# Another order for the prologue of a hybrid attention and MoE layer on eight cores

## The chip, the cores and the metric

The kernel runs on the 8 cores of one Trainium2 chip, all with the same program and each with its own part of the data. The cores don't wait for each other. The metric is the device time in microseconds (us) of the slowest core.

## What is computed

One layer, for 2 sequences of 8192 tokens of width 1024, conditioned by a vector `c` per sequence. The changed part prepares the first half of the layer:

```python
ada = jax.nn.silu(c) @ ada_w[l] + ada_b[l]                    # (B,6D)
sh1, sc1, g1, sh2, sc2, g2 = jnp.split(ada[:, None, :], 6, axis=-1)
h = rmsnorm(x, norm1_g[l]) * (1.0 + sc1) + sh1
proj = h @ w_in[l]                                            # (B,S,3072)
q, k, v, gb, gc, hc = jnp.split(proj, split_pts, axis=-1)
attn = diff_attention(q, k, v, positions, rel_bias, ...)      # causal, 2 softmax maps per head
conv = short_conv(gb, gc, hc, conv_w[l])
mix = jnp.concatenate([attn, conv], axis=-1) @ w_out[l]
x = x + g1 * mix
h = rmsnorm(x, norm2_g[l]) * (1.0 + sc2) + sh2
x = x + g2 * hier_moe(h, ...)
```

`rel_bias` gives each head a bias that depends only on the distance between query and key. It matters near the diagonal, and is applied there as a factor.

## The kernel before

Each core attends from 16 blocks of 128 own queries to all keys before them. It makes the keys (`KT`) and the values (`VA`) for its whole sequence itself, in 32 chunks of 256 tokens, and its queries in 8 chunks of 256. A chunk is a *unit*. The list `units` names them in order, and each has a place in one of three input buffers, `xb[u % 3]`. `load_unit(u + 3)` is issued on GpSimd's queue (POOL) when the last matmul of unit `u` is issued. Such a load casts float32 to bf16 on its way. `sq_unit(u + 1)` squares the next unit on VectorE (DVE) into the one tile `sq`, and is issued right behind the matmuls that take the statistics of unit `u` (`it_stat`), which read `sq`. So the place of a unit in the program also places the square of the next on DVE.

The order on each engine is that of the calls of `P.op`. An engine waits for the semaphores of an operation before it starts it, and everything behind it on that engine waits too. No planner moves anything.

The prologue is what comes before the first attention pair. In the program's order it is:

- SyncE's queue (SP) loads `ada_w` in pieces of 512 columns (`ada_ld`, two loads of 1 MB each). Pieces 2 and 3 make the scale `sc1`. Then come small tables, and the weights of keys and values into the staging tiles `wA` and `wB` (`w_ld`, 2 MB each).
- DVE multiplies pieces 2 and 3 with silu(c) (`gemv`, 8 operations a piece), and TensorE (PE) turns the result into columns (`to_cols`). The scale `der` comes of that.
- *Small tables*: DVE makes `rb0`, `Sm` and `c8`, PE multiplies them (`mmw`), ScalarE (ACT) takes the exponential, and DVE writes `w8b`. SP stores it to `wscr` in device memory. Then come lambda (`lamp`, `lams`), `identb` and a small memset on POOL.
- `cast_piece` scales `wA` and `wB` into `Wkv`, every second of the 16 slices on DVE and the others on ACT.
- SP loads the five *Hankel tiles* `Hs_l` from `wscr`: each has 128 partitions of 8 rows of 128 bf16, 256 bytes a row, with the start shifted by one element from partition to partition. Behind them on SP stand the *shift loads*: `ada_w` pieces 0 and 1 (for `sh1`), and the weights of the queries into `wA`.
- Keys and values of chunks 0 and 1, then `ada_piece(0)` and `ada_piece(1)` (the shift, which ends with the addition into `adaT`), chunk 2, `gq` (the shift times the query weights, for `bias_q`), the casts of `wA` into `Wq`, the keys of chunk 3, the five Hankel tiles through PE into `Mt`, `bias_q`, the queries of chunk 0, the values of chunk 3, and `gv` (for `bias_v`). Then the attention pairs begin.

In the tables below L344 is `ada_ld`, L348 `w_ld`, L328 `load_unit`, L332 `sq_unit`, L373 and L376 a `gemv`, L385 `to_cols`, L549 and L573 statistics and keys, L598 values, L632 and L655 statistics and projection of the queries, L450 and L454 the casts, L411 the first small table on DVE, L420 `mmw`, L467 the Hankel loads, L684 the addition into `adaT`, L702 the copies into `Mt`. L807, L815 and L818 are scores, exponential and the factor `Mt` of an attention pair.

## Time and profile before

| | |
|---|---|
| time, median of 3 runs | 1859.33 us (1854.24 to 1882.98) |
| the profiled execution's own time | 1857.9 us |
| its span, first to last instruction, slowest core (core 3) | 1856.4 us |
| spans of the eight cores | 1833.4 to 1856.4 us |
| busy on core 3: PE, DVE, ACT, POOL | 71%, 42%, 46%, 16% of the span |
| first attention scores on core 3 | at 119.58 us |

A time in the trace counts from the first instruction of its core. "Idle before, releaser" is how long an engine had waited, and for what. A row of SPq is the issue of a DMA, not its transfer. The prologue is the first 6% of the span, and everything after it is started by the attention loop.

### The profile page before, as it was taken

To read this page: it belongs to the slowest core of one execution; us is meant where nothing else is said; L and a number is where in the kernel's file an instruction comes from. 1 tells how busy PE (TensorE), PEld (TensorE's weight loads), DVE (VectorE), ACT (ScalarE), POOL (GpSimd) and SP (SyncE) were. 2 spreads that over 40 slices of the span, in tenths; PEclk is the share of its full clock that TensorE was granted. 3 is DMA by queue.
4 is the path that set the end of the run, shared out by engine and by line. 5 is a ranking of instruction groups with operands and counts; after the bars stand their busy time and mean duration, and the time that the engine had idled before them with its cause. 6 is when DMAs were issued, how large, how long until landed. Compare 5 with 4: busy or idle time off the path is not lost.

```text
span 1856.4 us, 41117 instructions; the slowest of 8 cores (1833.4 to 1856.4 us)
## 1 busy us (share of the span) xinstructions
PE 1311.5 (71%) x14526; PEld 880.3 (47%) x14526; DVE 779.5 (42%) x1229; ACT 846.6 (46%) x1122; POOL 303.3 (16%) x317
## 2 busy tenths in 40 slices
PE   1577777877888998899996268883156888888400
PEld 1354455565666676677775246661123433344200
DVE  4465455653333233223123377664612322233266
ACT  1134344555677887888885136652011221222122
POOL 0000000000000100001000043332311222222243
PEclk9788889999999999999998579996578999999855
DMA  8746556674455556656649844313158686421276
GB/s 224 187 94 140 115 121 136 151 174 64 80 80 96 94 87 95 102 84 100 95 78 199 227 131 128 103 58 108 68 191 288 215 287 212 165 90 37 92 230 222
DMA packets 120460, 252.88 MB, mean 136 GB/s; under 512 B 25643, under 2 KB 53019, under 8 KB 120264
## 3 DMA queue, kind: packets, MB, share of 16 engines
q0 software_dynamic: 30112, 96.50, 28.0%
q1 hardware_dynamic: 90152, 153.75, 26.5%
q8 instruction: 125, 2.05, 0.4%
q14 instruction: 71, 0.58, 0.1%
HBM read 400.89 MB, written 89.70 MB: 264 GB/s over the span
## 4 chain that ended last, share of the span: by engine, by line
PE 46%; issue 15%; DVE 13%; DMA 12%; ACT 10%; SPq 3%; POOL 1%; DVEq 0%; ACTq 0%; POOLq 0%
PE psd L838 9%; PE psd L1527 7%; ACT arena L815 6%; PE psd L573 5%; PE psd L598 5%; PE psd L807 5%; DMA wal<-wbf 5%; PE psd L1559 4%; PE psd L1204 2%; DMA arena<-w_in 2%; DMA arena<-ada_w 2%; DVE arena L1631 2%; PE psd L1165 1%; PE psd L655 1%; DVE arena L1185 1%
## 5 line engine op out<-in xcount | busy, mean ns | idle before, releaser
L815 ACT ACTIVATE arena<-psd,arena 128x1024 bf16<-128x1024 f32 x544 | 572.4, 1111 | 230.3 <-PE psd L809 214.3
L838 PE MATMUL psd<-arena 128*128 128x129 bf16 x4352 | 311.0, 226 | 12.4 <-DVE arena L818 10.1
L838 PEld LDWEIGHTS psd<-arena 128*128 128x128 bf16 x4352 | 283.7, 101 | 45.6 <-issue 14.7
L1527 PE MATMUL psd<-wal,arena 128*128 x752 | 195.5, 398 | 50.0 <-DMA wal<-wbf 30.9
L807 PE MATMUL psd<-arena 64*128 64x128 bf16 x2176 | 184.5, 218 | 28.5 <-ACT arena L815 22.1
L573 PE MATMUL psd<-arena 128*128 128x256 bf16 x1024 | 157.5, 292 | 45.5 <-ACT arena L557 18.9
L809 PE MATMUL psd<-arena 64*128 64x128 bf16 x2176 | 186.7, 219 | 0.4 <-issue 0.4
L807 PEld LDWEIGHTS psd<-arena 64*128 64x128 bf16 x2176 | 124.2, 94 | 104.4 <-issue 91.2
L598 PE MATMUL psd<-arena 128*128 128x512 bf16 x512 | 144.0, 385 | 30.6 <-DVE arena L611 10.9
L1527 PEld LDWEIGHTS psd<-wal,arena 128*128 128x128 bf16 x752 | 75.7, 101 | 169.3 <-issue 117.3
L1534 ACT ACTIVATE arena<-psd 128x512 f32<-128x512 f32 x47 | 28.1, 597 | 277.2 <-PE psd L1527 240.0
L481 POOL DMA_DIRECT2D wbf<-wex x96 | 50.0, 521 | 618.0 <-ACT arena L815 427.2
L611 DVE TENSOR_SCALAR arena<-psd,arena 128x512 bf16<-128x512 f32 x56 | 42.1, 752 | 234.5 <-PE psd L598 222.5
L573 PEld LDWEIGHTS psd<-arena 128*128 128x128 bf16 x1024 | 93.8, 104 | 76.4 <-issue 54.1
L809 PEld LDWEIGHTS psd<-arena 64*128 64x128 bf16 x2176 | 122.4, 95 | 1.6 <-issue 1.5
L1165 PE MATMUL psd<-arena 128*128 128x260 bf16 x768 | 99.3, 289 | 14.5 <-ACT arena L1170 12.2
L1559 PE MATMUL psd<-wal,arena 128*128 x376 | 88.7, 378 | 17.2 <-DVE arena L1547 15.2
L1547 DVE COPY arena<-psd 128x512 bf16<-128x512 bf16 x47 | 19.9, 424 | 180.2 <-PE psd L1544 150.8
L1570 POOL DMA_INDIRECT ysc<-arena x47 | 47.4, 1009 | 284.8 <-DVE arena L1567 273.4
L1567 DVE SCALAR_TENSOR_TENSOR arena<-psd,arena 128x1024 f32<-128x1024 f32 x47 | 60.3, 1284 | 76.0 <-PE psd L1559 74.5
L1165 PEld LDWEIGHTS psd<-arena 128*128 128x128 bf16 x768 | 77.1, 102 | 30.4 <-issue 15.2
L818 DVE TENSOR_TENSOR arena<-arena 128x1024 bf16<-128x1024 bf16 x79 | 53.1, 688 | 50.3 <-ACT arena L815 50.1
(222 smaller groups left out, 1585.7 us busy)
## 6 DMA issues: line engine op xcount, KB each, us to landing
wal<-wbf SPq DMA_DIRECT2D x300, 512.0 KB
wbf<-wex POOLq DMA_DIRECT2D x96, 512.0 KB, 5.5
arena<-ada_w SPq DMA_DIRECT2D x24, 1024.0 KB
arena<-xc POOLq DMA_DIRECT2D x32, 512.0 KB, 7.4
arena<-ysc SPq DMA_DIRECT2D x16, 1024.0 KB
arena<-w_in SPq DMA_DIRECT2D x12, 1024.0 KB
arena<-xo SPq DMA_DIRECT2D x16, 520.0 KB
arena<-xr SPq DMA_DIRECT2D x16, 512.0 KB
```

The source lines that it names most:

```text
L481: P.op("pool", lambda e: e.dma_start(out=wbf[pt][ex, :, :], in_=wex[ex, :, pt * PCW:(pt + 1) * PCW]), after=after, w=[("wbf", ex, pt)], dm ...
L573: ins = e.matmul(ps[:, m2 * 256:(m2 + 1) * 256], lhsT=Wkv[:, fc, mc * 128:(mc + 1) * 128], rhs=xbu[:, fc, :], start=(fc == 0), stop=(fc == ...
L598: ins = e.matmul(ps, lhsT=xbu[:, fc, t_ * 128:(t_ + 1) * 128], rhs=Wkv[:, fc, 512:1024], start=(fc == 0), stop=(fc == 7), skip_group_check ...
L807: e.matmul(sA[:, h * 128:(h + 1) * 128], lhsT=KT[0:64, h, kb * 128:(kb + 1) * 128], rhs=qt[0:64, h, q0:q0 + 128], start=True, stop=True)
L809: ins = e.matmul(sB[:, h * 128:(h + 1) * 128], lhsT=KT[64:128, h, kb * 128:(kb + 1) * 128], rhs=qt[64:128, h, q0:q0 + 128], start=True, st ...
L815: P.op("act", lambda e: e.activation(out=Pt[pb], in_=psd[sset][:, :], func=AF.Exp, scale=rk[:, kb:kb + 1]), r=[PSK(2 * sset), PSK(2 * sset ...
L818: P.op("dve", lambda e: e.tensor_tensor(out=Pt[pb], in0=Pt[pb], in1=Mt[:, gen, :], op=ALU.mult), r=[("Pt", pb), "Mt"], w=[("Pt", pb)])
L838: ins = e.matmul(omap(m), lhsT=Pt[pb][:, c * 512 + h * 128:c * 512 + (h + 1) * 128], rhs=VA[:, kb, h, :], start=(first and m % 3 == 0), st ...
L1165: ins = e.matmul(psb[bk][:, 0:260], lhsT=Wc[:, fc, br * 512 + cc * 128:br * 512 + (cc + 1) * 128], rhs=hnp[pp][:, fc, :, :], start=(fc == ...
L1527: ins = e.matmul(pd[:, :], lhsT=hT[b % 2][:, fc, :], rhs=ap_, start=(fc == 0), stop=(fc == 7))
L1559: ins = e.matmul(py[:, hf * 512:(hf + 1) * 512], lhsT=hidT[b % 2][:, jc, :], rhs=ap_, start=(jc == 0), stop=(jc == 3))
L1567: P.op("dve", lambda e: e.scalar_tensor_tensor(out=ysb[b % 2], in0=py[:, :], scalar=gateT[:, b:b + 1], in1=G2bc, op0=ALU.mult, op1=ALU.mul ...
```

## The change

Four things move, and no computation is added or taken away:

1. `cast_piece(wA)` and `cast_piece(wB)` stand ahead of the small tables, and the shift loads (`ada_ld(0, 0)`, `ada_ld(1, 2)`, `w_ld(wA, ...)`) right behind them.
2. The store to `wscr` and the five Hankel loads are issued by POOL instead of SP.
3. The first query chunk is the third unit instead of the fifth, and chunks 2 and 3 of the keys move back by one. Its statistics come ahead of the shift pieces, its projection right behind the Hankel tiles.
4. The casts into `Wq` are all on ACT (8) instead of 4 on DVE and 4 on ACT.

```diff
-    units = [("kv", c) for c in range(4)] + [("q", 0), ("q", 1)]
+    units = [("kv", 0), ("kv", 1), ("q", 0), ("kv", 2), ("kv", 3), ("q", 1)]
...
          r=["vec", "der"], w=["der"])
 
+    def cast_piece(stg, stgkey, dst, dcol, gcol, engs=("dve", "act"), width=512):
...
+    G1C = der[:, GSC1:GSC1 + 8]
+    cast_piece(wA, "wA", Wkv, 0, G1C)
+    cast_piece(wB, "wB", Wkv, 512, G1C)
...
+    ada_ld(0, 0)
+    ada_ld(1, 2)
+    w_ld(wA, "wA", 0)
     P.op("dve", lambda e: e.tensor_scalar(out=nb31, in0=nb31, scalar1=-1.0, scalar2=None, op0=ALU.mult),
          r=["nb31"], w=["nb31"])
...
-    P.op("sp", lambda e: e.dma_start(out=wscr[:, :], in_=w8b), r=["w8"], w=["wscr"], dma=True)
+    P.op("pool", lambda e: e.dma_start(out=wscr[:, :], in_=w8b), r=["w8"], w=["wscr"], dma=True)
...
-    G1C = der[:, GSC1:GSC1 + 8]
-    cast_piece(wA, "wA", Wkv, 0, G1C)
-    cast_piece(wB, "wB", Wkv, 512, G1C)
...
-        P.op("sp", lambda e, sp_=sp_, src=src: e.dma_start(out=Hs_l[sp_], in_=src), r=["wscr"], w=[("Hs", sp_)], dma=True)
-    ada_ld(0, 0)
-    ada_ld(1, 2)
-    w_ld(wA, "wA", 0)
+        P.op("pool", lambda e, sp_=sp_, src=src: e.dma_start(out=Hs_l[sp_], in_=src), r=["wscr"], w=[("Hs", sp_)], dma=True)
...
-    k2, v2 = kv_items(2, 2)
-    k3, v3_ = kv_items(3, 3)
-    for it in k0 + k1 + v0 + v1:
+    qi0 = q_items(2, 0)
+    k2, v2 = kv_items(3, 2)
+    k3, v3_ = kv_items(4, 3)
+    for it in k0 + k1 + v0 + v1 + qi0[0:1]:
         issue(it)
     ada_piece(0, 0)
     ada_piece(1, 2)
...
-    for it in k2 + v2:
-        issue(it)
     gq, _ = gemv(lambda kc: wA[:, kc, :], lambda kc: adaT[:, SH1 + kc:SH1 + kc + 1], lambda kc: ["wA", "adaT"])
-    cast_piece(wA, "wA", Wq, 0, der[:, GQ:GQ + 8])
-    for it in k3:
+    cast_piece(wA, "wA", Wq, 0, der[:, GQ:GQ + 8], ("act",))
+    for it in k2:
         issue(it)
     for sp_ in range(5):
...
-    for it in q_items(4, 0):
-        issue(it)
-    for it in v3_:
+    for it in qi0[1:] + v2 + k3 + v3_:
         issue(it)
```

The orders below are those of the two programs. In brackets stand the semaphores that an operation waits for: s_pe is PE's own count, and so on, and d with a number is one DMA's.

POOL before, from the third load of a unit on:

```order
L328 DMA arena<-xc 128x2048 [waits s_dve]
L444 MEMSET arena 128x32
L328 DMA arena<-xc 128x2048 [waits s_pe,d48]
L328 DMA arena<-xoq 128x2048 [waits s_pe,d49,s_dve]
L328 DMA arena<-xoq 128x2048 [waits s_pe,d50,s_dve]
```

POOL after, the same stretch, where L449 is the store to `wscr` and L470 the Hankel loads:

```order
L328 DMA arena<-xoq 128x2048 [waits s_dve]
L449 DMA wscr<-arena 8x768 [waits s_dve]
L465 MEMSET arena 128x32
L470 DMA arena<-wscr 128x8x128 [waits d51]
L470 DMA arena<-wscr 128x8x128 x4
L328 DMA arena<-xc 128x2048 [waits s_pe,d48]
L328 DMA arena<-xc 128x2048 [waits s_pe,d49,s_dve]
```

The load of unit 3 (the first that waits for s_pe) now stands behind six other DMAs in POOL's queue.

DVE before, from the last small table to the shift pieces, where L454 are the casts and L464 is `antib`:

```order
L443 CAST arena<-arena 128x128 [waits d13]
L454 TENSOR_SCALAR arena<-arena 128x512 [waits d14]
L454 TENSOR_SCALAR arena<-arena 128x512 x3
L454 TENSOR_SCALAR arena<-arena 128x512 [waits d15]
L454 TENSOR_SCALAR arena<-arena 128x512 x3
L464 CAST arena<-arena 128x128 [waits d12]
L332 TENSOR_TENSOR arena<-arena 128x2048 [waits s_pe,d49]
L332 TENSOR_TENSOR arena<-arena 128x2048 [waits s_pe,d50,s_dve]
L373 TENSOR_SCALAR arena<-arena 128x512 [waits d22]
```

DVE after, from the casts on (L419; L432 to L437 are the tables ahead of `mmw`, L448 is `w8b`):

```order
L419 TENSOR_SCALAR arena<-arena 128x512 [waits d15]
L419 TENSOR_SCALAR arena<-arena 128x512 x3
L432 TENSOR_SCALAR arena<-arena 8x1 [waits d10]
L434 TENSOR_TENSOR arena<-arena 32x8 [waits d8,d9]
L435 TENSOR_SCALAR arena<-arena 32x768 [waits d6,d7]
L437 TENSOR_SCALAR arena<-arena 8x768
L448 TENSOR_TENSOR arena<-arena 8x768 [waits s_act,s_dve]
...
L332 TENSOR_TENSOR arena<-arena 128x2048 [waits s_pe,d49]
L332 TENSOR_TENSOR arena<-arena 128x2048 [waits s_pe,d50,s_dve]
L332 TENSOR_TENSOR arena<-arena 128x2048 [waits s_dve,s_pe,d57]
L373 TENSOR_SCALAR arena<-arena 128x512 [waits d16]
```

The casts moved ahead of the tables, and a third square, that of unit 3 (it waits for d57, the load of unit 3), now stands ahead of the first shift piece.

PE before, from the end of the key chunk 3 on:

```order
L698 MATMUL psd<-arena 128x512 [waits s_dve,d21]
L699 MATMUL psd<-arena 128x512
L385 MATMUL psd<-arena 128x1 [waits s_dve]
L385 MATMUL psd<-arena 128x1 x3
L632 MATMUL psd<-arena 128x256 [waits s_act]
L632 MATMUL psd<-arena 128x256 x7
L655 MATMUL psd<-arena 128x256 [waits s_act,d52]
```

PE after, behind the last Hankel tile:

```order
L697 MATMUL psd<-arena 128x512 [waits s_dve,d56]
L698 MATMUL psd<-arena 128x512
L385 MATMUL psd<-arena 128x1 [waits s_dve]
L385 MATMUL psd<-arena 128x1 x3
L655 MATMUL psd<-arena 128x256 [waits d50,s_act]
...
L598 MATMUL psd<-arena 128x512 [waits s_act]
L598 MATMUL psd<-arena 128x512 x7
...
L549 MATMUL psd<-arena 128x1 [waits s_dve]
L549 MATMUL psd<-arena 128x1 x15
L573 MATMUL psd<-arena 128x256 [waits s_act,d58]
```

Values of chunk 2 and the whole of chunk 3 moved behind the Hankel tiles, and the statistics of the queries moved ahead of them. `mmw` stays where it was on PE, ahead of the first statistics and keys.

## Rows read from the trace of the kernel before

**Rows 1.** Spans and mean granted TensorE clock of the two cores that ended last.

```profile
core 3: 1856.4 us, clock 0.890
core 4: 1855.3 us, clock 0.890
```

**Rows 2.** Timeline of core 3, 33 to 59 us: start, length, operation, idle before.

```profile
33.40 0.14 DVE L411 TENSOR_SCALAR arena<-arena 8x1 f32<-8x1 f32 x1
34.93 1.86 PE L420 MATMUL psd<-arena 32*8 32x512 f32 x2 [2.63 <-DVE arena L414]
37.57 0.59 PE L549 MATMUL psd<-arena 128*128 128x1 bf16 x16
42.92 3.25 DVE L454 TENSOR_SCALAR arena<-arena 128x512 bf16<-128x512 f32 x8
44.20 8.60 SPq L467 DMA_DIRECT2D arena<-wscr  x5
44.85 5.84 PE L573 MATMUL psd<-arena 128*128 128x256 bf16 x32 [6.69 <-DVE arena L454]
46.22 1.22 DVE L332 TENSOR_TENSOR arena<-arena 128x2048 bf16<-128x2048 bf16 x1
52.90 8.29 SPq L344 DMA_DIRECT2D arena<-ada_w  x4
58.64 0.53 POOL L328 DMA_DIRECT2D arena<-xc  x1 [27.01 <-PE psd L598]
```

**Rows 3.** Timeline of core 3, the shift pieces and the wait of ACT beside them.

```profile
66.98 0.49 DVE L373 TENSOR_SCALAR arena<-arena 128x512 f32<-128x512 f32 x1 [14.44 <-DMA arena<-ada_w]
86.76 0.16 DVE L684 TENSOR_TENSOR arena<-arena,psd 128x8 f32<-128x8 f32 x1 [2.10 <-PE psd L385]
87.17 0.17 ACT L557 ACTIVATE arena<-psd 128x2 f32<-128x2 f32 x1 [24.89 <-PE psd L549]
```

**Rows 4.** Timeline of core 3, from the keys of chunk 3 to the first pairs.

```profile
95.92 3.65 PE L573 MATMUL psd<-arena 128*128 128x256 bf16 x32
100.11 1.49 DVE L702 CAST arena<-psd 128x512 bf16<-128x512 f32 x2 [2.53 <-PE psd L699]
107.58 1.84 PE L385 MATMUL psd<-arena 128*128 128x1 f32 x8 [1.41 <-DVE arena L702]
109.28 1.87 PE L632 MATMUL psd<-arena 128*128 128x256 bf16 x8
116.03 3.62 PE L598 MATMUL psd<-arena 128*128 128x512 bf16 x16
124.02 2.49 DVE L818 TENSOR_TENSOR arena<-arena 128x1024 bf16<-128x1024 bf16 x4
```

**Rows 5.** DMA queues of core 3, 0 to 44 us: packets, MB, share of 16 engines.

```profile
q1 hardware_dynamic: 5120, 8.81, 64.4%
```

**Rows 6.** Timeline of core 4: second half of the casts, both shift pieces.

```profile
46.14 1.68 DVE L454 TENSOR_SCALAR arena<-arena 128x512 bf16<-128x512 f32 x4 [1.45 <-DMA arena<-w_in]
72.95 0.49 DVE L373 TENSOR_SCALAR arena<-arena 128x512 f32<-128x512 f32 x1 [20.93 <-DMA arena<-ada_w]
87.92 0.16 DVE L684 TENSOR_TENSOR arena<-arena,psd 128x8 f32<-128x8 f32 x1 [2.09 <-PE psd L385]
```

**Rows 7.** Landing of the unit loads of core 3 in its first 300 us.

```profile
DMA to landing us min/median/max: 5.2/8.6/12.1
```

**Rows 8.** DMA queues of core 3, 44 to 60 us.

```profile
q1 hardware_dynamic: 5213, 1.39, 64.0%
```

**Rows 9.** DMA queues of core 6, 42 to 51 us.

```profile
q1 hardware_dynamic: 5201, 1.41, 74.0%
```

**Rows 10.** Busy time of core 3 by stretch; the last three are PE clock, DMA share, GB/s.

```profile
20.00:24.00 4.00, 1.07 (x6) 1.10 (x6) 3.69 (x6) 0.00 (x0) 0.00 (x0) 1.00 1.02 329
```

**Rows 11.** DMA queues of core 3, 68 to 70 us.

```profile
q0 software_dynamic: 80, 0.27, 76.0%
q1 hardware_dynamic: 79, 0.16, 27.4%
```

More of the change, by code:

```diff
@@ L419, in mmw @@
-    def mmw(e):
-        e.matmul(psb[2][0:8, 0:512], lhsT=rb0[:, :], rhs=Sm[:, 0:512], start=True, stop=True)
-        return e.matmul(psb[3][0:8, 0:256], lhsT=rb0[:, :], rhs=Sm[:, 512:768], start=True, stop=True)
-    P.op("pe", mmw, r=["rb0", "Sm"], w=[PSK(2), PSK(3)])
-    P.op("act", lambda e: e.activation(out=w8[:, 0:512], in_=psb[2][0:8, 0:512], func=AF.Exp, bias=nb31[:, 0:1], scale=1.0),
-         r=[PSK(2), "nb31"], w=["w8a"])
-    P.op("act", lambda e: e.activation(out=w8[:, 512:768], in_=psb[3][0:8, 0:256], func=AF.Exp, bias=nb31[:, 0:1], scale=1.0),
-         r=[PSK(3), "nb31"], w=["w8b"])
@@ L444, in build_program @@
-    P.op("pool", lambda e: e.memset(VA[:, 0:8, :, 128:129], 1.0), w=["va1"])
     def cast_piece(stg, stgkey, dst, dcol, gcol, engs=("dve", "act"), width=512):
@@ new lines, in build_program, with mmw @@
+    P.op("dve", lambda e: e.tensor_scalar(out=c8, in0=dv32[0:8, :], scalar1=0.0, scalar2=None, op0=ALU.is_ge),
+         r=["dv32"], w=["c8"])
+    def mmw(e):
+        e.matmul(psb[2][0:8, 0:512], lhsT=rb0[:, :], rhs=Sm[:, 0:512], start=True, stop=True)
+        return e.matmul(psb[3][0:8, 0:256], lhsT=rb0[:, :], rhs=Sm[:, 512:768], start=True, stop=True)
+    P.op("pe", mmw, r=["rb0", "Sm"], w=[PSK(2), PSK(3)])
+    P.op("act", lambda e: e.activation(out=w8[:, 0:512], in_=psb[2][0:8, 0:512], func=AF.Exp, bias=nb31[:, 0:1], scale=1.0),
+         r=[PSK(2), "nb31"], w=["w8a"])
@@ new lines, in build_program @@
+    P.op("dve", lambda e: e.tensor_reduce(out=lams, in_=lamp.rearrange("p (a d) -> p a d", a=2), axis=AX.X,
+                                          op=ALU.add), r=["lamp"], w=["lams"])
+    P.op("act", lambda e: e.activation(out=lams, in_=lams, func=AF.Exp), r=["lams"], w=["lams"])
+    P.op("dve", lambda e: e.scalar_tensor_tensor(out=der[:, LAMC:LAMC + 1], in0=lams[:, 0:1], scalar=LAM_INIT,
+                                                  in1=lams[:, 1:2], op0=ALU.add, op1=ALU.subtract),
+         r=["lams"], w=["derl"])
@@ new lines, in build_program @@
+    P.op("dve", lambda e: e.tensor_scalar(out=der[:, NLAM:NLAM + 1], in0=der[:, LAMC:LAMC + 1], scalar1=-1.0, scalar2=None,
+                                          op0=ALU.mult), r=["derl"], w=["dernl"])
+    P.op("dve", lambda e: e.tensor_scalar(out=der[:, OML:OML + 1], in0=der[:, NLAM:NLAM + 1], scalar1=1.0, scalar2=None,
+                                          op0=ALU.add), r=["dernl"], w=["deroml"])
+    P.op("dve", lambda e: e.tensor_copy(out=identb, in_=ident), r=["ident"], w=["identb"])
@@ L464, in build_program @@
+    P.op("pool", lambda e: e.memset(VA[:, 0:8, :, 128:129], 1.0), w=["va1"])
     P.op("dve", lambda e: e.tensor_copy(out=antib, in_=antiid), r=["antiid"], w=["antib"])
```

35 lines of the change are left out of this document (12 added, 23 removed).

## Prediction

> **What bounds the kernel now.** I read the spans of the cores first: cores 3 and 4 end last, at 1856.4 and 1855.3 us [rows 1]. The cores don't wait for each other, so the time falls only if these two get faster, and rises with whichever ends last. After the prologue all work hangs on the attention loop, in which nothing waits for a fixed time. I take it that a shift of the first pairs reaches the end one for one. Then I read the timeline of the prologue of core 3 and look for the wait that ends last at each step.
>
> It has one large hole. DVE waits 14.44 us for `ada_w` until 66.98 us [rows 3], since SP issued these loads only at 52.90, behind the Hankel loads that it had started at 44.20 [rows 2]. The addition into `adaT`, from here on **T**, is at 86.76 [rows 3], and PE and ACT have little to do until then: ACT waited 24.89 us. This is the hole that an earlier issue of the shift loads addresses. The question is what is late next.
>
> **The shift loads (part 1).** SP now issues them right behind `wB`. One queue hands its transfers over in order: between 44 and 60 us the queue moved 5213 packets and 1.39 MB [rows 8], which is the five Hankel tiles (5 x 1024 rows of 256 bytes, 1.31 MB) and hardly anything of the `ada_w` loads issued from 52.90 on. So `wB` keeps its place and the 6.3 MB behind it (4.2 MB `ada_w`, 2.1 MB `wA`) start when it has landed, at **W**. For core 3, 8.81 MB had moved by 44 us [rows 5], all that SP had issued; I take W = 43.5. At 329 GB/s [rows 10] the 4.2 MB take 12.7 us. They are there by about 57 on core 3, 10 us before DVE got the first of them in the trace. If nothing else were in the way, DVE would start the pieces then, and T would come 14.97 us later [rows 6], at 72: earlier by some 15 us. Something is.
>
> **The tables behind the casts (part 1).** DVE now does the small tables after the casts of `wB`, and PE's order still has `mmw` ahead of the first keys. Before, the tables were done while the weights were on their way. Now they come after W: four casts, half of the 3.25 us [rows 2], 1.7 with the gap; from L411 to L420 1.53 us; from L420 to the statistics 2.64 us, and 0.6 for these [rows 2]. The first keys start at W + 6.5 = 50.0 on core 3, against 44.85 [rows 2]: 5.2 us later. On core 4 the second casts waited for `wB` until 46.14 [rows 6], so its keys start near 52.6. The square of unit 1 waits behind the tables too. It was done at 47.44, 12.5 us after L420; without the 3.25 us of casts that stood between, it is done 9.4 us after L420, at 56.2, when PE has needed it since 55.8. Take 0.6 us for it.
>
> **The third unit (part 3).** The load of unit 3 is issued when the values of chunk 0 are done, 13.8 us after the first keys (58.64 less 44.85) [rows 2]. That becomes 50.0 + 13.8 + 0.6 = 64.4 on core 3. Before, nobody needed this unit before T. Now its square stands ahead of the first shift piece on DVE, so both shift pieces wait for unit 3. Once it has landed, at **S**, come a square (1.22 us) [rows 2] and the two pieces with PE's part, 14.97 us from 72.95 to 87.92 on core 4, where nothing held them up on the way [rows 6]: T = S + 16.3.
>
> **POOL's queue (part 2).** The six new DMAs stand ahead of the load of unit 3 on POOL. The first Hankel load went out 9.3 us after L420 [rows 2]; L420 is now at 46.8, so they go out near 56. They need a way through the engines too. Core 3 took the 15 us from 44.6 to 59.7 for them, with the queue to itself [rows 8]; core 6 needed some 8.5 us [rows 9], so this differs between cores. Two queues share the engines by turns: from 68 to 70 us the unit load moved 80 packets and the `ada_w` load 79 [rows 11]. So I count one Hankel packet for one 2 KB packet of SP's queue. By 56 us SP's queue has moved 4.1 of its 6.3 MB. The other 1070 packets and as many of the Hankels take 9.5 us (6.7 at the full rate and 2.8 for the small ones), to 65.5. The remaining 4100 Hankel packets need 12.2 us at the rate of [rows 8], to 77.7, and 6.7 at that of [rows 9], to 72.2. Unit 3 stands in the same queue behind them and takes another 2 us: S = 79.7, or 74.2. If the Hankels were no hindrance, S would be 64.4 + 5.2, the shortest landing [rows 7], 69.6. Core 3 has shown the slow rate itself, so I take 79.7.
>
> How long POOL's own share of a Hankel load takes, no row shows. Its unit loads take 0.53 us [rows 2], with 128 rows each; a Hankel load has 1024. So a load costs between 0.53 us and eight times that, 4.2 us, or five of them 3 to 21 us; a gain is excluded, since POOL did none of it before. I take the low end, at which the drain above hides it. The high end is a rival. The Trainium skill, "DMA: Bandwidth & Descriptors", section "Anatomy of one DMA", says that many descriptors can be emitted before their cost shows; no row here shows it.
>
> **The sum up to T.** Core 3: 79.7 + 16.3 = 96.0 against 86.76, **+9.2**. Core 4, with W = 46.1, 2.6 us later in everything: 98.6 against 87.92, **+10.7**.
>
> **Behind T.** `gq` no longer waits behind a square, the four Wq casts leave DVE (1.7 us), and only one chunk of keys stands ahead of the Hankel tiles instead of two with values. ACT takes four more casts while it is idle for 24.89 us [rows 3]; without that cover they would cost 2.8 us. The copies into `Mt` start when `gq` (6.4 us, half of the 14.97 less PE's 2.1) and a square are done, at T + 8, against 100.11 - 86.76 = 13.4 [rows 4]. That gives 5.4 us, and it is given back at once. Behind the Hankel tiles PE had the statistics (1.7 us), the queries, and values of one chunk. Now it has the queries, values of two chunks, and statistics and keys of one: 3.5 + 0.6 + 3.65 - 1.7 = +6.0 us [rows 4]. The scores start 0.6 us later after T. (In steps: copies at T + 8, `to_cols` 7.5 us behind their start, the queries 1.7 us behind that, and done 5.05 us later, at T + 22.2.) The exponentials have less to wait for: before, the first factor `Mt` on DVE waited for `gv` until 124.02, T + 37.3. Now `gv` waits for the square of unit 5, whose load goes out when the queries are done (T + 22.2) and lands 5.2 us later: T + 27.6, the square to T + 29, `gv` to T + 35.5. The pairs then go at ACT's pace, and I put the whole at **-0.5**.
>
> **The result of the sum.** Core 4 ends at 1855.3 + 10.2 = 1865.5, core 3 at 1856.4 + 8.7 = 1865.1: +9.1 on the span, 1867.0 for the profiled execution's 1857.9. The median of the runs is 1.4 above that execution, which is within their spread of 1854 to 1883. I forecast **1867**.
>
> **Rivals.**
>
> *Turns of many packets.* If the Hankels get as many bytes a turn as the large packets, they are limited only by their own rate from 56 us on: 15 us to 71 on core 3, and S = 73. T = 89.3, +2.5 and -0.5: +2.0. Core 4 would come to +4.1 - 0.5, and end at 1858.9: about 1860. Against it stand the 80 and 79 packets of [rows 11], though both kinds there were large. The Trainium skill, "DMA: Bandwidth & Descriptors", section "Queues, rings and completion order", says that an engine changes between its queues only after a packet of some 9 to 17 descriptors. By that rule the Hankels take turns of about 4 KB, and this rival is the likelier one; the trace of large packets can't decide between them.
>
> *The Hankels are out of the way.* The drain goes at core 6's rate or faster, or overlaps fully. Then S = 69.6 and T = 85.9 on core 3 (-0.9) and 88.5 on core 4 (+0.6): 1858. For it: 8.5 us on core 6 [rows 9]. Against: core 3, one of the two that end last, had the slow rate.
>
> *Faster, because the weights land early.* All of the above hangs on W. If `wB` lands at 40 instead of 43.5 to 46, and the Hankels are out of the way, T falls by 4 to 6 us on both last cores, and the time is about 1853. Nothing in the change makes `wB` earlier, but it differs between cores by some us.
>
> *Slower, POOL's descriptor work.* At 4.2 us a Hankel load, POOL is busy with them from 56 to 77, and unit 3 goes out after that: S = 77 + 5.2 = 82.2 on core 3 and 84.8 on core 4. T = 101.1 there, +13.2 - 0.5: 1870, and with a drain that starts late as well about 1876. It decides from 1.7 us a load on, where POOL would be busy until 64.4, when unit 3 could go. It is slower than before, by under 2%.
>
> That the change doesn't do what it says is excluded by the orders shown: POOL issues the Hankels, and SP's shift loads stand right behind `wB`.
>
> **How the numbers follow.** The forecast 0.40, turns of many packets 0.25, out of the way 0.13, early weights 0.07, POOL's work 0.12, something larger outside the prologue 0.03. The range goes from the early side of "out of the way" to POOL's work with its late drain: 1855 to 1877. A measurement of this kernel tells about 2% (37 us) from no change. No case but the last reaches that. The prologue is 120 us, and its largest hole 14 us. So: faster by over 2% 0.01, within 0.96, slower 0.03.
>
> **What would show it.** In the profile after, on cores 3 and 4: first keys at 50 to 53 us instead of 45; no wait for `ada_w` on DVE; in its place a wait of the third square for the load of unit 3, until 74 to 80; T at 90 to 98; then a wait of some 10 us less ahead of the copies into `Mt` and longer PE work behind them; first scores 33 to 34 us after T. POOL's rows for the Hankels should be under 1.7 us each. I am wrong if T comes below 85 on the last cores, if the drain of the Hankels takes under 10 us beside the other queue, or if the distance from T to the end changes by more than 3 us.

## The result, and the profile after

The changed kernel takes 1877.0 us (median of 4 runs, 1876.9 to 1877.8) and the kernel before 1859.3 (median of 3). The ratio is 1.010, with a 95% interval of 1.007 to 1.013. So it is slower by 1%, which is less than the 2% bound. The time, 1877.01, lies at the very edge of the range of 1855 to 1877 and 10 us above the forecast, and the change is about twice the 9.1 us that the sum had. Some executions have a lower clock on one die and take longer: all times here are medians without them, and of `e2_hankel_sp` and `e10_units_only`, whose profiled execution had cores 4 to 7 at a granted clock of 0.87 to 0.88, only the prologue is used.

The spans of the cores in the profiled execution, first core 1, then the two that ended last before [rows 1], and core 6:

```profile
core 1: 1845.0 us, clock 0.892
...
core 3: 1841.0 us, clock 0.897
core 4: 1876.2 us, clock 0.884
...
core 6: 1840.6 us, clock 0.894
```

Core 4 is 20.9 us longer, core 3 is 15.4 shorter. The prologue explains only half of the first, and it has the opposite sign for the second. So start with core 4, where the steps of the prediction can be compared one by one. Its timeline up to the Hankel loads (start, length, operation, idle before; before it was [rows 6], and [rows 2] on core 3):

```profile
36.19 1.67 DVE L419 TENSOR_SCALAR arena<-arena 128x512 bf16<-128x512 f32 x4 [2.20 <-DMA arena<-w_in]
45.35 1.67 DVE L419 TENSOR_SCALAR arena<-arena 128x512 bf16<-128x512 f32 x4 [7.49 <-DMA arena<-w_in]
47.83 1.86 PE L441 MATMUL psd<-arena 32*8 32x512 f32 x2 [14.99 <-DVE arena L435]
50.92 5.93 PE L573 MATMUL psd<-arena 128*128 128x256 bf16 x32
54.66 0.54 POOL L449 DMA_DIRECT2D wscr<-arena  x1 [22.73 <-DVE arena L454]
61.66 4.46 POOL L470 DMA_DIRECT2D arena<-wscr  x5 [6.21 <-DMA wscr<-arena]
66.10 0.58 POOL L328 DMA_DIRECT2D arena<-xc  x1
```

`wB` landed by 45.35. The tables (L441) come behind its casts, and the first keys (L573) start at 50.92. The store to `wscr` goes out at 54.66, and POOL then waits 6.21 us for it to land. It issues the five Hankel loads from 61.66 on, 4.46 us for all, and unit 3 at once behind them. The same core from there to the first pairs:

```profile
81.84 1.22 DVE L332 TENSOR_TENSOR arena<-arena 128x2048 bf16<-128x2048 bf16 x1 [22.39 <-DMA arena<-xc]
82.98 0.48 DVE L373 TENSOR_SCALAR arena<-arena 128x512 f32<-128x512 f32 x1
98.00 0.16 DVE L685 TENSOR_TENSOR arena<-arena,psd 128x8 f32<-128x8 f32 x1 [2.09 <-PE psd L385]
105.86 1.48 DVE L701 CAST arena<-psd 128x512 bf16<-128x512 f32 x2
121.12 3.62 PE L598 MATMUL psd<-arena 128*128 128x512 bf16 x16
132.76 4.12 ACT L812 ACTIVATE arena<-psd,arena 128x1024 bf16<-128x1024 f32 x4
```

DVE no longer waits for `ada_w` (20.93 us in [rows 6]). In its place the third square waits 22.39 us for its load, the shift pieces follow, and T is at 98.00 instead of 87.92. On core 3 the same two rows stand earlier:

```profile
75.19 1.23 DVE L332 TENSOR_TENSOR arena<-arena 128x2048 bf16<-128x2048 bf16 x1 [17.45 <-DMA arena<-xc]
91.36 0.16 DVE L685 TENSOR_TENSOR arena<-arena,psd 128x8 f32<-128x8 f32 x1 [2.09 <-PE psd L385]
```

The chain of waits of core 4, followed back from its end, runs through just this place:

```profile
54.66 6.44 DMA wscr<-arena
61.66 3.35 POOL arena L470 x4
65.23 0.88 POOL arena L470
66.10 15.64 DMA arena<-xc
```

Its DMA queues from 66 to 82 us (kind: packets, MB, share of 16 engines), under the line that sorts the packets by size:

```profile
DMA packets 614, 2.09 MB, mean 131 GB/s; under 512 B 105, under 2 KB 105, under 8 KB 613
...
q0 software_dynamic: 613, 2.08, 87.5%
```

SP's queue is through by then. What keeps unit 3 is POOL's own queue. These 2.08 MB are most of the Hankel tiles (1.31 MB) and two unit loads (1.05 MB), and they get only 131 GB/s on this core, against the 329 of [rows 10].

**Where the other cores stand.** The first exponential, from here on E, is the last point before the attention loop. It was at 120.3 on core 3 and 122.3 on core 4, and is now at 126.3 and 132.8: +6.0 and +10.5. Now core 1, before:

```profile
44.15 4.33 SPq L467 DMA_DIRECT2D arena<-wscr  x5
60.26 0.49 DVE L373 TENSOR_SCALAR arena<-arena 128x512 f32<-128x512 f32 x1 [9.21 <-DMA arena<-ada_w]
80.61 0.16 DVE L684 TENSOR_TENSOR arena<-arena,psd 128x8 f32<-128x8 f32 x1 [2.09 <-PE psd L385]
114.56 4.12 ACT L815 ACTIVATE arena<-psd,arena 128x1024 bf16<-128x1024 f32 x4
```

and after:

```profile
80.80 1.23 DVE L332 TENSOR_TENSOR arena<-arena 128x2048 bf16<-128x2048 bf16 x1 [20.21 <-DMA arena<-xc]
96.98 0.16 DVE L685 TENSOR_TENSOR arena<-arena,psd 128x8 f32<-128x8 f32 x1 [2.09 <-PE psd L385]
130.69 4.12 ACT L812 ACTIVATE arena<-psd,arena 128x1024 bf16<-128x1024 f32 x4
```

Core 1 had its Hankels out of SP's queue in 4.33 us instead of core 3's 8.60 [rows 2], and its shift loads early. The change took 16.1 us from it. Cores 1, 2, 5 and 6 were of this kind in that execution: +16.1, +16.8, +18.6 and +19.8 at E. The other four lost 4.4 to 10.5. The mean over the eight cores is 117.2 before and 129.6 after, **+12.4 us**, and not the +8.7 and +10.2 of the two cores in the sum.

Which cores are quick changes from one execution to the next. In `e4_delay`, whose program is that of the kernel before up to the shift pieces, it was cores 0, 3, 5 and 7 that issued the Hankels in 4.2 to 4.6 us, and cores 1, 2, 4 and 6 that took 7.7 to 9.2. Core 3, slow in [rows 2], and then core 1, quick above:

```profile
44.20 4.58 SPq L467 DMA_DIRECT2D arena<-wscr  x5
...
47.78 8.81 SPq L467 DMA_DIRECT2D arena<-wscr  x5
```

### The profile page after: what moved, and what is told of

The parts are those of the page before. It is cut to its first block, busy times and chain, and to the rows that moved or that the text cites. A ratio compares the mean times of both kernels' runs of the same rounds, so it can differ in the third digit from the quotient of the medians.

```text
span 1876.2 us, 41125 instructions; the slowest of 8 cores (1840.6 to 1876.2 us)
## 1 busy us (share of the span) xinstructions
PE 1324.8 (71%) x14526; PEld 884.7 (47%) x14526; DVE 774.5 (41%) x1225; ACT 848.1 (45%) x1126; POOL 307.1 (16%) x323
## 4 chain that ended last, share of the span: by engine, by line
PE 45%; issue 16%; DVE 13%; DMA 10%; ACT 9%; SPq 4%; POOL 1%; DVEq 1%; ACTq 0%; POOLq 0%
PE psd L835 9%; PE psd L1524 7%; PE psd L573 5%; PE psd L598 5%; ACT arena L812 5%; PE psd L804 5%; DMA wal<-wbf 5%; PE psd L1556 4%; PE psd L1201 2%; DMA arena<-w_in 2%; PE psd L655 2%; PE psd L1162 1%; DVE arena L1628 1%; DVE arena L1182 1%; DVE arena L376 1%
## 5 line engine op out<-in xcount | busy, mean ns | idle before, releaser
L804 PE MATMUL psd<-arena 64*128 64x128 bf16 x2176 | 187.5, 221 | 29.5 <-ACT arena L812 24.1
L806 PE MATMUL psd<-arena 64*128 64x128 bf16 x2176 | 189.3, 222 | 0.1
L573 PE MATMUL psd<-arena 128*128 128x256 bf16 x1024 | 161.8, 298 | 37.1 <-ACT arena L557 17.2
L804 PEld LDWEIGHTS psd<-arena 64*128 64x128 bf16 x2176 | 126.8, 96 | 109.0 <-issue 96.6
L573 PEld LDWEIGHTS psd<-arena 128*128 128x128 bf16 x1024 | 95.8, 105 | 70.3 <-issue 47.2
L806 PEld LDWEIGHTS psd<-arena 64*128 64x128 bf16 x2176 | 125.0, 96 | 0.3 <-issue 0.3
L1162 PE MATMUL psd<-arena 128*128 128x260 bf16 x768 | 97.8, 286 | 15.3 <-ACT arena L1167 12.9
L815 DVE TENSOR_TENSOR arena<-arena 128x1024 bf16<-128x1024 bf16 x79 | 53.2, 688 | 52.6 <-ACT arena L812 52.4
```

The source lines that it names most:

```text
L573: ins = e.matmul(ps[:, m2 * 256:(m2 + 1) * 256], lhsT=Wkv[:, fc, mc * 128:(mc + 1) * 128], rhs=xbu[:, fc, :], start=(fc == 0), stop=(fc == ...
L804: e.matmul(sA[:, h * 128:(h + 1) * 128], lhsT=KT[0:64, h, kb * 128:(kb + 1) * 128], rhs=qt[0:64, h, q0:q0 + 128], start=True, stop=True)
L806: ins = e.matmul(sB[:, h * 128:(h + 1) * 128], lhsT=KT[64:128, h, kb * 128:(kb + 1) * 128], rhs=qt[64:128, h, q0:q0 + 128], start=True, st ...
L815: P.op("dve", lambda e: e.tensor_tensor(out=Pt[pb], in0=Pt[pb], in1=Mt[:, gen, :], op=ALU.mult), r=[("Pt", pb), "Mt"], w=[("Pt", pb)])
L1162: ins = e.matmul(psb[bk][:, 0:260], lhsT=Wc[:, fc, br * 512 + cc * 128:br * 512 + (cc + 1) * 128], rhs=hnp[pp][:, fc, :, :], start=(fc == ...
```

## The experiments

In the expectations K is the start of the first keys, T the addition into `adaT`, E the first exponential, and "rest" the span less E. The table has their means over the eight cores of each profiled execution. The last column is the mean over the cores' spans and over all runs used, less that of the kernel before on the same chip. In the 61 runs of the kernel before used there, the mean of a run scatters by some 3 us (standard deviation), while its last core stands 5 to 22 us above that mean.

| kernel | K | T | E | rest | median us | ratio, 95% | mean of spans, less before |
|---|---|---|---|---|---|---|---|
| before | 45.0 | 83.3 | 117.2 | 1728.8 | | | |
| changed | 51.0 | 95.2 | 129.6 | 1722.5 | 1877.0 | 1.007 to 1.013 | +11.9 |
| e5_changed_again | 51.0 | 93.5 | 127.9 | 1724.2 | 1869.2 | 1.005 to 1.012 | +12.8 |
| e9_square_behind | 51.0 | 78.6 | 112.3 | 1718.6 | 1847.7 | 0.996 to 1.002 | -6.4 |
| e1_units_back | 50.9 | 74.3 | 108.5 | 1727.3 | 1854.4 | 0.995 to 1.000 | -6.8 |
| e2_hankel_sp | 52.1 | 92.0 | 126.8 | | 1867.5 | 1.004 to 1.008 | +9.5 |
| e3_tables_first | 44.9 | 88.8 | 122.8 | 1726.9 | 1863.6 | 1.000 to 1.005 | +3.0 |
| e10_units_only | 44.6 | 84.2 | 119.2 | | 1858.0 | 1.001 to 1.004 | +0.6 |
| e6_shift_first | 44.5 | 66.8 | 100.9 | 1721.8 | 1833.8 | 0.986 to 0.992 | -14.9 |
| e7_sp_order_only | 44.7 | 67.5 | 114.3 | 1723.9 | 1850.8 | 0.997 to 1.003 | +0.4 |
| e4_delay | 45.0 | 95.3 | 125.5 | 1726.4 | 1863.4 | 1.002 to 1.006 | +4.5 |
| e8_keys_in_hole | 44.6 | 71.9 | 99.9 | 1721.6 | 1835.4 | 0.987 to 0.992 | -17.9 |
| e11_split_columns | 44.6 | 69.4 | 98.8 | 1724.8 | 1835.9 | 0.990 to 0.994 | -18.8 |
| e12_copies_on_both | 44.5 | 69.2 | 97.4 | 1722.6 | 1840.9 | 0.990 to 0.996 | -15.1 |

Beside e1 to e4 the kernel before took 1858.8 us (median of 29 runs), beside e5 to e8 1853.5 (15), beside e9 to e12 1852.5 (17). The +11.9 of the changed kernel is the mean of its four runs (1857.9) less the one execution of the kernel before whose cores are known there (1846.0).

`e5_changed_again` is the changed kernel once more, on another chip. If the prologue is the whole loss, its ratio was expected near 1.0067; if the changed kernel loses some 5 us more behind the prologue, its time was expected near 1877 again, with a longer rest than the others have. The ratio is 1.009, the time 1869.2, and the rest, 1724.2, is within that of the others.

### What holds T: e1_units_back and e9_square_behind

The forecast says that the third square, with its load behind the Hankels, holds T. e1 keeps everything of the change but the order of the units:

```diff
-    units = [("kv", 0), ("kv", 1), ("q", 0), ("kv", 2), ("kv", 3), ("q", 1)]
+    units = [("kv", c) for c in range(4)] + [("q", 0), ("q", 1)]
...
-    for it in k0 + k1 + v0 + v1 + qi0[0:1]:
+    for it in k0 + k1 + v0 + v1:
```

> The changed kernel with the old order of units (the query chunk fifth, chunk 2 of the keys third) and all else as changed. Theory A (the third unit): the shift pieces are late in the changed kernel because the square of unit 3 stands ahead of them on DVE and its load lands late. Without it DVE starts them when the square of unit 2 is done and the ada_w load is there, near 60 us, and the addition into adaT comes near 76 us on all cores instead of 91 to 98. The first exponential comes some 18 to 22 us earlier than in the changed kernel, and the time is near 1857, at or below the kernel before. Theory B (the drain of the Hankel loads and the tables behind the casts are the loss in themselves, whatever the order of units): the addition stays above 88 us and the time above 1870.

T came at 74.3 and E at 108.5, 21 us before the changed kernel, and the time is 1854.4 us, 4 us under the kernel before. e9 is the sharper test. It leaves all loads and queues as the change has them, and on DVE only moves the square behind the products of both shift pieces:

```diff
-    for it in k0 + k1 + v0 + v1 + qi0[0:1]:
+    for it in k0 + k1 + v0 + v1:
         issue(it)
-    ada_piece(0, 0)
-    ada_piece(1, 2)
+    sh = [gemv(... ada_h[hs + kc // 4] ...)[0] for hs in (0, 2)]
+    issue(qi0[0])
+    for pc in range(2):
+        to_cols(sh[pc], 7, pc * 4, [("ps7ada", pc)], ["adaTs"])
```

> The changed kernel with one thing moved: the statistics of the query chunk, and with them the square of unit 3 on DVE, stand behind the two gemv of the shift (PE's columns come behind the statistics). Units, tables, casts and POOL's queue stay as changed. Theory A (the third square ahead of the shift pieces turns the late landing of unit 3 into the loss): DVE starts the pieces near 60 us, the addition into adaT comes near 76 instead of 93 to 95 in the mean, the first exponential near 110 instead of 128 to 130, and the mean of the cores' spans falls by 17 to 19 us, to some 6 under the kernel before. Theory H (the square only moves the wait, since the keys of unit 3 need its load as well): the first exponential comes at 122 or later.

Timeline of core 4 in e9:

```profile
61.53 0.48 DVE L373 TENSOR_SCALAR arena<-arena 128x512 f32<-128x512 f32 x1
...
68.00 0.52 DVE L373 TENSOR_SCALAR arena<-arena 128x512 f32<-128x512 f32 x1
...
80.38 1.23 DVE L332 TENSOR_TENSOR arena<-arena 128x2048 bf16<-128x2048 bf16 x1 [5.87 <-DMA arena<-xc]
81.52 0.15 DVE L688 TENSOR_TENSOR arena<-arena,psd 128x8 f32<-128x8 f32 x1
```

The square itself is as late as in the changed kernel, at 80.38, but the pieces are done in the hole, and the addition follows the square at once. E falls by 17.3 us (15.6 against e5). This one position on DVE turns a loss of 12.8 in the mean of spans into a gain of 6.4. That the third square holds T is shown.

### What each part costs: e2_hankel_sp, e3_tables_first, e10_units_only

e2 sends the Hankel loads through SP's queue, behind the shift loads and `wA`:

```diff
-        P.op("pool", lambda e, sp_=sp_, src=src: e.dma_start(out=Hs_l[sp_], in_=src), ...
+        P.op("sp", lambda e, sp_=sp_, src=src: e.dma_start(out=Hs_l[sp_], in_=src), ...
```

> The changed kernel with the five Hankel loads back on SP's queue, behind the shift loads and the query weights; the store to wscr stays on POOL. Theory A: the load of unit 3 is late because the Hankel loads stand ahead of it in POOL's queue. Alone in that queue it is issued at some 64 to 66 us and lands 5 to 9 us later, so the wait of the third square ends near 73 instead of 75 to 82, and the addition into adaT comes near 90 on all cores: 6 us earlier on those that had 96 to 98, 1 or 2 on the others; time near 1872. Theory C (the engines are full, it doesn't matter which queue has the Hankels): the square ends its wait where it did, within 2 us, and the time stays at 1877.

E is 2.8 us earlier, though K happened to be 1.1 later in this execution. e3 keeps POOL's queue and moves the casts back behind the small tables:

```diff
-    cast_piece(wA, "wA", Wkv, 0, G1C)
-    cast_piece(wB, "wB", Wkv, 512, G1C)
...
-    ada_ld(0, 0)
-    ada_ld(1, 2)
-    w_ld(wA, "wA", 0)
     P.op("dve", lambda e: e.tensor_scalar(out=nb31, in0=nb31, scalar1=-1.0, scalar2=None, op0=ALU.mult),
...
+    cast_piece(wA, "wA", Wkv, 0, G1C)
+    cast_piece(wB, "wB", Wkv, 512, G1C)
...
+    ada_ld(0, 0)
+    ada_ld(1, 2)
+    w_ld(wA, "wA", 0)
     P.op("dve", lambda e: e.tensor_copy(out=antib, in_=antiid), r=["antiid"], w=["antib"])
```

> The changed kernel with the small tables ahead of the casts again. Theory A: the first keys start 5 us earlier, near 45 to 47, and so does the load of unit 3; the Hankel loads go out some 8 us earlier too. The addition into adaT comes 5 to 8 us earlier, the time is near 1870. Theory D (the landing of unit 3 is set by the end of all transfers, not by its issue): the keys start earlier, but the third square waits until the same time as in the changed kernel, and the time stays within 2 us of 1877.

K is back at 44.9, and E 6.8 us earlier. e10 does both, so that of the change only the early shift loads and the new order of the units are left (with the store to `wscr` on POOL and the Wq casts on ACT, as in the change):

> Tables first and Hankel loads on SP as in e6_shift_first, but the new order of units kept. Of the changed kernel it has parts 3 and 4 and the early shift loads, and none of the two things that made its unit 3 late. Theory A: unit 3 is issued near 58.6 and lands near 68, the third square ends its wait there, the addition comes near 84 in the mean (e6: 67, before: 83), the first exponential near 118, and the time is within 3 us of the kernel before: the new order of units alone costs the 16 us that the early shift loads bring. If the order of units is harmless once the queues are clear, the first exponential is near 101 as in e6.

E is 119.2, 2.0 later than before. The early shift loads bring nothing here, since DVE still waits, as core 4 shows:

```profile
66.78 1.23 DVE L332 TENSOR_TENSOR arena<-arena 128x2048 bf16<-128x2048 bf16 x1 [15.95 <-DMA arena<-xc]
...
82.88 0.16 DVE L685 TENSOR_TENSOR arena<-arena,psd 128x8 f32<-128x8 f32 x1 [2.09 <-PE psd L385]
```

The load is issued at 56.94 there and has no Hankels ahead of it in POOL's queue. Its square still comes at 66.78. So the new order is dear even without the queue: it costs about what the early loads bring.

### The good part alone: e6_shift_first and e7_sp_order_only

e6 is e10 with the old order of the units. Against the kernel before:

```diff
-    P.op("sp", lambda e: e.dma_start(out=wscr[:, :], in_=w8b), r=["w8"], w=["wscr"], dma=True)
+    P.op("pool", lambda e: e.dma_start(out=wscr[:, :], in_=w8b), r=["w8"], w=["wscr"], dma=True)
...
+    ada_ld(0, 0)
+    ada_ld(1, 2)
+    w_ld(wA, "wA", 0)
     P.op("dve", lambda e: e.tensor_copy(out=antib, in_=antiid), ...
     for sp_ in range(5):
...
         P.op("sp", ... e.dma_start(out=Hs_l[sp_], in_=src), ...
-    ada_ld(0, 0)
-    ada_ld(1, 2)
-    w_ld(wA, "wA", 0)
...
-    cast_piece(wA, "wA", Wq, 0, der[:, GQ:GQ + 8])
+    cast_piece(wA, "wA", Wq, 0, der[:, GQ:GQ + 8], ("act",))
```

> Old order of units and of the tables; SP issues the shift loads and the query weights ahead of the Hankel loads, the store to wscr goes by POOL. It is the one part of the change that the hole in the profile asks for. Theory A: first keys stay at 45 us, DVE starts the shift pieces near 56 to 58, the addition into adaT comes near 72 (before: 83 in the mean), the first exponential near 106 (before: 117), and the time is 9 to 11 us under the kernel before. Theory F (with the shift early, the Hankel loads behind 6.3 MB are the next late thing and hold up the copies into Mt): the first exponential comes at 112 or later and the gain is under 5 us.

Core 4 of e6:

```profile
47.68 26.50 SPq L470 DMA_DIRECT2D arena<-wscr  x5
...
53.22 0.48 DVE L373 TENSOR_SCALAR arena<-arena 128x512 f32<-128x512 f32 x1
...
67.61 0.16 DVE L685 TENSOR_TENSOR arena<-arena,psd 128x8 f32<-128x8 f32 x1 [1.45 <-PE psd L385]
...
101.44 4.12 ACT L814 ACTIVATE arena<-psd,arena 128x1024 bf16<-128x1024 f32 x4
```

The first shift piece starts at 53.22 with no wait, where it started at 72.95 [rows 6]. T is at 66.8 in the mean, earlier than expected. The time is 1833.8 us, 0.986 to 0.992 of the kernel before: by 1.1% it beats both kernels.

These kernels take the change apart. At E: before to e6 -16.3 (the large loads early, with the store on POOL and the casts on ACT), e6 to e10 **+18.3** (order of the units), e10 to e3 **+3.6** (Hankels through POOL's queue), e3 to the changed kernel **+6.8** (tables behind the casts). These steps lead from the kernel before to the changed one, so they add up to +12.4 by construction. On cores 0 to 3 alone the second and third term are 17.3 and 4.7. The other way round gives about the same: e1 differs from the changed kernel by 21.1 for the units, e2 from e10 by 7.6 for the tables. The two profiled executions of the changed kernel differ by 1.7 us at E (129.6 and 127.9), and each other kernel has only one, so a term is good to about 2 at best.

e7 asks how little suffices: the two shift loads move ahead of the store, and all else, `wA` too, stays as before.

```diff
+    ada_ld(0, 0)
+    ada_ld(1, 2)
     P.op("sp", lambda e: e.dma_start(out=wscr[:, :], in_=w8b), r=["w8"], w=["wscr"], dma=True)
...
-    ada_ld(0, 0)
-    ada_ld(1, 2)
     w_ld(wA, "wA", 0)
```

> The kernel before with ada_ld(0, 0) and ada_ld(1, 2) moved ahead of the store to wscr on SP, nothing else. One queue hands its transfers over in order, so the small store should land behind 4.2 MB, near 57 us instead of 43 to 50; the Hankel loads go out then, and the query weights behind them land near 80. The shift addition comes near 72, but gq waits for the query weights until about 80: first exponential near 113, gain 3 to 5 us. If instead the store lands within 5 us of its issue, queues are not in order, the weights land near 65 and the first exponential comes near 106.

T is at 67.5, as in e6, but E is 13.4 us behind it, and the time is that of the kernel before (0.997 to 1.003). Core 4 shows where the gain went:

```profile
58.08 14.64 SPq L469 DMA_DIRECT2D arena<-wscr  x5
...
67.37 0.16 DVE L684 TENSOR_TENSOR arena<-arena,psd 128x8 f32<-128x8 f32 x1 [1.28 <-PE psd L385]
...
90.29 0.49 DVE L373 TENSOR_SCALAR arena<-arena 128x512 f32<-128x512 f32 x1 [17.95 <-DMA arena<-w_in]
```

The Hankels stand ahead of the query weights on SP, and `gq` now waits 17.95 us for them. In e6 all three large loads go ahead of the small rows, and this wait is gone. But e7 differs from e6 in two more things: the store to `wscr` stays on SP, where it waits its turn behind 4.2 MB, so that the Hankels go out at 58.08 instead of 47.68, and half of the Wq casts stay on DVE. What each of the three is worth no run separates.

### What a late T is worth: e4_delay

e4 leaves the kernel before alone and puts two more products on DVE ahead of the addition, 12.9 us of work that nobody uses. It separates lateness from every queue.

```diff
+    for _ in range(2):
+        gemv(lambda kc: ada_h[2 + kc // 4][:, kc % 4, :], lambda kc: vec[:, CP + kc:CP + kc + 1], ...)
     P.op("dve", lambda e: e.tensor_tensor(out=adaT[:, 0:8], in0=adaT[:, 0:8], in1=psb[7][:, 0:8], op=ALU.add),
```

> The kernel before with 16 more operations on DVE (two more gemv over the second shift piece, results not used) ahead of the addition into adaT: a pure delay of the prologue of 12.9 us on every core, with nothing else changed. It asks how a shift of the prologue reaches the time. Theory A: one for one. The mean of the cores' spans rises by 12 to 13 us and the time to 1873, as in the changed kernel whose first exponential is 12.5 us later in the mean of the cores. Theory E (the attention loop takes part of a delay back, and the changed kernel loses more time behind the prologue): the time rises by clearly less than 12 us, say to 1866.

T came 12.0 us later and E 8.3, the mean of spans only 4.5. A part was got back, since E follows T by 30.2 us here instead of 33.9: in the delay PE did keys that otherwise come behind T. So less than the delay reached the end, and behind E one for one did not hold in this run either. In e5 it did, about: +10.7 at E and +12.8 in the mean of spans. Between E and the mean of spans the exchange was thus 0.5 to 1.2, and 0.9 in e6 (14.9 of 16.3). Each of these ratios has its E from one execution, so how much of their spread is chance stays open.

### The first measurement again: e5_changed_again

The changed kernel as it is, in another call:

> The changed kernel once more, beside the others of this call. Its four runs lay 16 to 18 us over the kernel before, while its first exponential is only 12.4 us later in the mean of the cores. Theory A (the prologue is the whole loss, and those four runs had a late last core by chance): the ratio is near 1.0067, a median near 1871 to 1873. Theory E (the changed kernel loses some 5 us more behind the prologue): the median is again near 1877 and the mean time from the first exponential to the end is longer than the 1722 to 1729 us of the other kernels.

It is 16.5 us above the kernel before, as at first (16.2). The mean of the spans rose by 12.8. The remaining 3 or 4 us are the distance of the last core from the mean: 14 us in the kernel before over 61 runs, 17 and 19 in the 4 runs each of the changed one, 10 to 17 in the others. Whether this is chance in eight runs or belongs to the change, no run here settles.

### Further on: e8_keys_in_hole, e11_split_columns, e12_copies_on_both

With T at 67 DVE and PE wait in turn for the square of unit 3 and for the columns. e8 puts keys and values of chunk 2 between the products and the columns:

```diff
-    ada_piece(0, 0)
-    ada_piece(1, 2)
+    sh = [gemv(... ada_h[hs + kc // 4] ...)[0] for hs in (0, 2)]
+    for it in k2 + v2:
+        issue(it)
+    for pc in range(2):
+        to_cols(sh[pc], 7, pc * 4, [("ps7ada", pc)], ["adaTs"])
...
-    for it in k2 + v2:
-        issue(it)
```

> e6_shift_first, and the keys and values of chunk 2 on PE ahead of to_cols of the shift pieces, while DVE does the two gemv first and the square of unit 3 only behind them. PE has about 9 us of work for the time in which it waits for the shift. Theory A: the addition stays near 72, the copies into Mt start about 7 to 8 us behind it instead of 13, and the first exponential comes 8 to 9 us earlier than in e6, near 97 to 99; time near 1841 to 1843. Theory G (the square of unit 3 or its load, behind the gemv, holds up gq as the third square did in the changed kernel): the first exponential is less than 4 us earlier than in e6.

I had missed a wait. On core 4 the square waits for its load, and the addition for PE, which has the values ahead of the columns:

```profile
67.37 1.23 DVE L332 TENSOR_TENSOR arena<-arena 128x2048 bf16<-128x2048 bf16 x1 [2.37 <-DMA arena<-xc]
...
72.86 0.16 DVE L689 TENSOR_TENSOR arena<-arena,psd 128x8 f32<-128x8 f32 x1 [4.26 <-PE psd L385]
```

T is 5 us later than in e6 and E only 1 earlier. e11 puts the columns, and the addition, between the keys and the values. Against e8:

```diff
-    for it in k2 + v2:
+    for it in k2:
         issue(it)
     for pc in range(2):
         to_cols(sh[pc], 7, pc * 4, [("ps7ada", pc)], ["adaTs"])
...
+    for it in v2:
+        issue(it)
```

> e8_keys_in_hole with to_cols between the keys and the values of chunk 2. In e8 the addition came 5 us later than in e6 because PE did the values first. Expected: addition near 69, copies into Mt 8 us behind it near 77 (e6: 81), first exponential near 96 to 97 against 100.9 in e6 and 99.9 in e8; mean of the cores 4 us under e6. If the square of unit 3 (its load lands near 68) is what holds up gq, the gain over e8 is under 1.5 us.

E is at 98.8, 2.1 before e6, about half of what I had hoped for. The mean of spans, 3.9 under that of e6, is as expected. e12 is e11 with every second copy into `Mt` on ACT, in two pieces:

```diff
+            if hh == 0:
+                P.op("dve", ... e.tensor_copy(out=mo, in_=mi), ...)
+            else:
+                for c_ in range(2):
+                    P.op("act", ... e.activation(out=mo[:, c_, :, :], in_=mi[:, c_, :, :], func=AF.Copy), ...)
```

> e11_split_columns, and half of the ten copies of the Hankel tiles into Mt on ACT (in two pieces each) instead of all on DVE, which paces PE there at 1.66 us a tile. Expected: 1.0 to 1.3 us a tile, the stretch from the first copy to bias_q 2 to 3 us shorter, first exponential near 94, time near 1830. If ACT is busy with the Wq casts or its two pieces take longer than DVE's two copies, nothing is gained.

E is at 97.4, where 94 was expected, and the time is no better. The three take 1835.4 to 1840.9 us, and e6 1833.8. In the mean of spans e8 and e11 lie 3.0 and 3.9 us lower than e6, on five and four runs, and e11 on another chip. I would keep e6: the others are not told apart from it here, and they are more to maintain.

## Why the prediction missed

**Right, on the two cores of the sum.** W was put at 43.5 and 46.1 and came at 43.6 and 45.3. The keys were put at 50.0 and 52.6 and came at 49.2 and 50.9. Unit 3 was to go out at 64.4 on core 3 and went at 64.22 (more on that below). In place of the wait for `ada_w` came a wait of the third square, which e9 shows to be the cause of the late T. The copies start 7.9 us behind T on core 4 (put at 8). E is 35.0 and 34.8 behind T, against 33.6 and 34.4 before: +1.4 and +0.4, where I had -0.5. POOL's rows for the Hankels are under 1.7 us. At E the sum said +8.7 and +10.2, and +6.0 and +10.5 were measured.

**The step that failed** is the first: "The cores don't wait for each other, so the time falls only if these two get faster, and rises with whichever ends last." The sum was made for cores 3 and 4 alone, and I took it that their shift reaches the end one for one. That they don't wait for each other holds, but the two that ended last in one execution do not stand for the time, and for single cores the shift does not reach the end one for one. The prediction had named a sign of being wrong here, a distance from T to the end that changes by more than 3 us: on core 3 it fell by 20.0 us, on core 4 it grew by 10.8, and in the mean of the eight it fell by 5.8.

Among 29 further runs of the kernel before, core 4 ends last 12 times, core 5 five times, core 1 four, cores 0 and 7 three each, core 3 twice. Behind E core 3 needed 1736.1 us before and 1714.7 after, core 4 1733.0 and 1743.4; the granted clock of [rows 1], 0.890 on both, is 0.897 and 0.884 after. One execution's last core is thus no property of the kernel. What a change moves is all eight cores, and the mean at E rose by 12.4.

The rows of core 6 [rows 9] had shown me the other kind of core: its Hankels were through in 8.5 us, and it had the more to lose. I used them only as a bound for the drain. With +12.4 the forecast would have been 1870, 3 us more. The other 7 us are the last core's distance from the mean of the eight: 10.4 us in the execution that I started from, and 17.7 in the mean of the four changed runs (11.1 to 24.1). A part of this is chance of the starting point, since that distance is 12.5 us in the mean of the 29 further runs; in e5 it is 15.7, beside 13.0 for the kernel before on that chip. Whether the changed kernel spreads its cores more, or four runs happened to, no run decides.

**The drain of the Hankels** was right in its end and wrong on the way. I counted one Hankel packet for one large one, up to 77.7 on core 3. But POOL's queue takes many rows into a packet. Its queue on core 3 from 60 to 64.2 us, when only Hankels stood in it:

```profile
q0 software_dynamic: 103, 0.36, 39.8%
```

These are 3.5 KB a packet, some 14 rows of 256 bytes, where SP's queue had 5213 packets for 1.39 MB [rows 8], about one a row. This is the first half of the rival "turns of many packets". The Trainium skill, "DMA: Bandwidth & Descriptors", section "Queues, rings and completion order", gives some 9 to 17 descriptors for a packet; the trace agrees on POOL's queue, and on SP's it doesn't. It did not make the load of unit 3 early, for two reasons. The store to `wscr` took 6.4 us to land on core 4, and POOL went on 6.8 and 7.0 us after issuing it, so that the Hankels went out at 59.8 on core 3 and 61.7 on core 4 instead of 56 and 58.6. And POOL's queue, alone from 66 us on, moved only 174 GB/s on core 3 (to 74 us) and 131 on core 4, so that unit 3 needed 11.0 us on core 3 and 15.7 on core 4 from its issue to the square. S came to 75.2 and 81.8, against 79.7 and 82.3 put, and 73 on core 3 for that rival. (My sum had a slip of 0.4 us there: at the rate that it uses for the 4100 packets, the 1070 before them take 3.2 us, and not 2.8.)

**The other rivals.** "POOL's descriptor work" is excluded as the cause: 0.89 us a load, against the 1.7 from which it would decide. But it held unit 3 a little. Before, the unit load went out 4.2 us after the first values began; now POOL is busy with the Hankels up to 64.24 us on core 3 and 66.12 on core 4, and the load goes right behind them, 4.6 and 4.8 us after the first values. That it went at the 64.4 that the sum had is in part luck, since the first keys were 0.8 us early. "Out of the way" is excluded: no core needed less than 11.0 us from the issue of unit 3 to its square, where that rival has 5.2. "Early weights" found no weights early. A loss behind the prologue (0.03) does not show: the rest is 1722.5 and 1724.2 in the changed kernel, and 1728.8 in the kernel before.

**The terms of the parts.** The tables behind the casts were put at 5.2 us and are worth 6.8 at E. The order of the units, which I had only as "in its place", is the largest term by far: 17 to 18 us even without the Hankels in POOL's queue. I had worked out that the third square stands ahead of the shift pieces, but not what T would be with the pieces ahead of it, and so had not seen that the change takes back its own gain of 16.3.

## What to carry to other kernels

Where the time is that of the slowest of several independent cores, make the sum for all of them, the quick ones above all: the last core of one execution is partly chance, and the mean of the cores moves with the change more steadily. When a load is brought forward, look for what now stands ahead of its use in the program order of the engine that waited for it; one square in the wrong place cost about as much here (16 to 18 us) as the early loads brought (16). Send large loads ahead of many small rows in a queue, all of them: with one left behind, and the store on the same queue (e7), nearly the whole gain went back.
